# Half of GpSimd's descriptor space given to two more places for expert rows

## The reference, cut to what matters

```python
def peer_ffn(h, wq, sub_keys, u, v):
    def block(t):
        q = (t @ wq).reshape(PEER_BLOCK, PEER_HEADS, 2, PEER_DQ // 2)
        s = jnp.einsum('tpcd,pckd->tpck', q, sub_keys).astype(jnp.float32)
        s1, i1 = lax.top_k(s[:, :, 0], PEER_TOPK)
        s2, i2 = lax.top_k(s[:, :, 1], PEER_TOPK)
        ...
        top, pos = lax.top_k(cand, PEER_TOPK)
        idx = jnp.take_along_axis(cidx, pos, axis=-1)
        g = jax.nn.softmax(top, axis=-1)
        a = jax.nn.gelu(jnp.einsum('tpkd,td->tpk', u[idx], t).astype(jnp.float32), approximate=False)
        return jnp.einsum('tpk,tpkd->td', (g * a).astype(t.dtype), v[idx])
```

## Time and profile before

| | us |
|---|---|
| median of 3 runs | 2861.39 |
| lowest, highest | 2847.32, 2865.62 |
| the profiled execution | 2850.39 |
| its span, first to last instruction | 2848.5 |

### The profile page before, as it was taken

How to read it: one execution, slowest core, us unless ns; L and a number is a source line. 1 busy time by engine, 2 the same in 40 slices (tenths; PEclk the granted TensorE clock), 3 DMA queues, 4 the chain that set the end, 5 groups by cost and what they waited for, 6 DMA issues and landing times.

```text
span 2848.5 us, 43514 instructions
## 1 busy us (share of the span) xinstructions
PE 2307.4 (81%) x16384; PEld 1723.0 (60%) x16384; DVE 1885.7 (66%) x4182; ACT 903.9 (32%) x1615; POOL 1095.7 (38%) x1029
## 2 busy tenths in 40 slices
PE   7999988877455564665757989766999999999998
PEld 5788876445311110113646877523777899997998
DVE  3666885787565666457898877663444587677766
ACT  4556652111100000001023334322423455457544
POOL 0000002544466666667786665676556000000000
PEclk8999999988787776877969999867999999999999
DMA  7432126797799999999999999999999545662554
GB/s 301 151 129 85 38 83 247 279 350 294 289 375 378 365 368 352 358 354 345 409 344 403 401 408 409 408 360 362 363 405 395 208 153 194 190 208 90 186 188 152
DMA packets 225231, 810.32 MB, mean 284 GB/s; under 512 B 24704, under 2 KB 30720, under 8 KB 223232
## 3 DMA queue, kind: packets, MB, share of 16 engines
q0 software_dynamic: 147456, 536.94, 49.3%
q1 hardware_dynamic: 76992, 270.09, 26.5%
q10 hardware_dynamic: 576, 0.52, 0.1%
HBM read 805.35 MB, written 2.10 MB: 283 GB/s over the span
## 4 chain that ended last, share of the span: by engine, by line
PE 39%; DVE 17%; issue 10%; DMA 8%; another core or an unknown queue 6%; POOL 3%; ACT 1%; DVEq 0%; POOLq 0%; SPq 0%; ACTq 0%
PE ps L2005 10%; PE ps L2006 9%; PE ps L2007 9%; DVE pe_ring L2848 6%; PE ps L1940 5%; DMA pe_ring<-in_v,pe_vidx 4%; DMA pe_ring<-in_u,pe_idx 1%; POOL pe_ring L1827 1%; PE ps L1895 1%; DVE pe_itop L2775 1%; POOL pe_ring L1833 1%; DVE la_w_lo L2901 1%; DVE pe_top L2771 1%; DMA la_k<-in_v,pe_vidx 1%
## 5 line engine op out<-in xcount | busy, mean ns | idle before, releaser
L1827 POOL DMA_INDIRECT pe_ring<-in_u,pe_idx x415 | 463.8, 1118 | 293.0 <-issue 113.3
L1940 PE MATMUL ps<-pe_ring,pe_spot 128*32 128x512 f32 x1620 | 386.9, 752 | 199.2 <-DMA pe_ring<-in_v,pe_vidx 140.9
L1833 POOL DMA_INDIRECT pe_ring<-in_v,pe_vidx x405 | 426.5, 1053 | 221.5 <-issue 116.4
L2005 PE MATMUL ps<-la_h_hi,la_w_hi 128*128 128x256 f32 x1696 | 483.4, 285 | 12.1 <-DVE la_w_lo L2901 6.7
L2007 PE MATMUL ps<-la_h_hi,la_w_lo 128*128 128x256 f32 x1696 | 477.8, 282 | 1.7 <-issue 1.7
L2006 PE MATMUL ps<-la_h_lo,la_w_hi 128*128 128x256 f32 x1696 | 477.6, 282 | 1.6 <-issue 1.5
L2901 DVE TENSOR_TENSOR la_w_lo<-la_w_raw,la_w_hi 128x1024 fp32r<-128x1024 f32 (+1 forms) x348 | 415.5, 1195 | 78.0 <-ACT la_w_hi L2470 64.1
L2470 ACT ACTIVATE la_w_hi<-la_w_raw 128x1024 fp32r<-128x1024 f32 (+1 forms) x348 | 359.5, 1033 | 295.4 <-DMA la_w_raw<-in_down 78.7
L2005 PEld LDWEIGHTS ps<-la_h_hi,la_w_hi 128*128 128x128 f32 x1696 | 323.2, 191 | 47.8 <-issue 31.7
L1940 PEld LDWEIGHTS ps<-pe_ring,pe_spot 128*32 128x32 f32 x1620 | 76.9, 125 | 411.9 <-issue 313.1
L2007 PEld LDWEIGHTS ps<-la_h_hi,la_w_lo 128*128 128x128 f32 x1696 | 320.3, 189 | 2.2 <-issue 2.1
(11 more groups left out here) (409 smaller groups left out, 3899.2 us busy)
## 6 DMA issues: line engine op xcount, KB each, us to landing
la_w_raw<-in_gate SPq DMA_DIRECT2D x88, 512.0 KB
la_w_raw<-in_up SPq DMA_DIRECT2D x88, 512.0 KB
la_w_raw<-in_down SPq DMA_DIRECT2D x64, 448.0 KB
la_w_raw<-in_a_in SPq DMA_DIRECT2D x40, 512.0 KB
wring<-in_w_in SPq DMA_DIRECT2D x32, 512.0 KB
la_w_raw<-in_down SPq DMA_DIRECT2D x32, 512.0 KB
wring<-in_wq SPq DMA_DIRECT2D x22, 512.0 KB, 7.5
xT<-in_w_mod_rows SPq DMA_DIRECT2D x8, 1024.0 KB, 4.9
```

The lines of the kernel that those rows point to most:

```text
L1827: pool.indirect_dma_start(row(n), None, io["u"], bass.IndirectOffsetOnAxis(idx[:, t, j:j + 1], 0)).then_inc(land[GATHERS[n][0]], 16)
L1833: pool.indirect_dma_start(row(n), None, io["v"], bass.IndirectOffsetOnAxis(vidx[:, t % 2, at:at + 1], 0)).then_inc(land[GATHERS[n][0]], 16)
L1940: return pe.matmul(ps[PER * grp:PER * grp + PER, half, :], spot[:, j // TOKENS % 2, grp, lo:lo + PER], row(n)[:, half * 512:(half + 1) * 5 ...
L2005: pe.matmul(slot(n), parts_hi[:, n % SPLIT, i, :], hi[:, k, :], start=first, stop=False)
```

## The change

The space for descriptors of GpSimd's dynamic DMAs is 8192 bytes of each partition, and the 8192 bytes that come free hold two further places for gathered rows, `pe_more_rows`, numbers `RING + 10` and `RING + 11`. They are lent from gather 0 to the end and need no wait at their first use (the last test in `slot_free` is cut to the places of `htok`). As each place has a semaphore of its own, three semaphores of the first stage (`x_in`) are now given back at that stage's end and cleared with the others. The diff, whole:

```diff
--- before.py
+++ after.py
@@ -65,6 +65,8 @@
     return [int(np.argmax(bucket >= b)) if (bucket >= b).any() else MAXD for b in range(BUCKETS)] + [MAXD]
 
 
+SCRATCH = 8192
+SPARE = (16384 - SCRATCH) // (4 * D)
 LN_EXP = "natural_log_exp_and_others"
 
 
@@ -244,7 +246,7 @@
                 return (first_ring if m < M_FIRST else later_ring)[m % 4].rearrange("p (k n) -> p k n", n=MODW if m < M_FIRST else D)
 
             c_in, c_ready, mod_dotted = stage_sem("na_c_in"), stage_sem("na_c_ready"), stage_sem("na_mod_dotted")
-            consts_in, x_in, mod_in = sem("consts_in"), [sem(f"x_in{n}") for n in range(3)], [sem(f"mod_in{u}") for u in range(4)]
+            consts_in, x_in, mod_in = sem("consts_in"), [stage_sem(f"x_in{n}") for n in range(3)], [sem(f"mod_in{u}") for u in range(4)]
             padded, silu_ready, x_squared, x_added, x_rooted = [stage_sem(f"na_{x}") for x in ("padded", "silu_ready", "x_squared", "x_added", "x_rooted")]
             mod_used, mod_evac, mod_summed, gained = sem("mod_used"), sem("mod_evac"), sem("mod_summed"), sem("mod_gained")
             x_full, projected_, staged = stage_sem("na_x_full"), stage_sem("na_projected"), stage_sem("na_staged")
@@ -1363,6 +1365,7 @@
     iota16 = sb("pe_iota16", [P, TOPK + 1], on=local)
     HT = T // 2
     work = sb("la_work", [P, 10 * HT], on=local)
+    more_rows = sb("pe_more_rows", [P, SPARE, D], on=local)
     flat = lambda x: x.rearrange("p a n -> p (a n)")
     s_of = [x.rearrange("p (h s n) -> p h s n", h=PE_H, s=2) for x in
             (work[:, 0:2 * D], flat(yT[:, 0:4, :]), flat(yT[:, 4:8, :]), wring[:, 4 * D:6 * D])]
@@ -1502,8 +1505,10 @@
     TOKEN_SLOTS, TOKENS_AT, LENT_AT = [RING + 9, RING + 8, RING + 6, RING + 7], 80, 11
     MORE = [(RING + k, TURN["v", 0, 0], TURN["v", 1, P - 1] + 1) for k in range(4)] + [(RING + 4, 0, KEPT), (RING + 5, 0, KEPT)]
     MORE += [(TOKEN_SLOTS[t], LENT_AT, TOKENS_AT if t else P) for t in reversed(range(TT))] + [(TOKEN_SLOTS[t], TURN["v", t, 16], len(ORDER)) for t in (2, 3)]
+    MORE += [(RING + 10 + k, 0, len(ORDER)) for k in range(SPARE)]
     row_spaces = ([ring[:, k, :] for k in range(RING)] + [within("hT", f"pe_more{k}", k * D, [P, D])[:, :] for k in range(4)]
-                  + [kT[:, :, :].rearrange("p a n -> p (a n)"), v[:, :, :, :].rearrange("p c t n -> p (c t n)"), htok[:, 2, :], htok[:, 3, :], htok[:, 1, :], htok[:, 0, :]])
+                  + [kT[:, :, :].rearrange("p a n -> p (a n)"), v[:, :, :, :].rearrange("p c t n -> p (c t n)"), htok[:, 2, :], htok[:, 3, :], htok[:, 1, :], htok[:, 0, :]]
+                  + [more_rows[:, k, :] for k in range(SPARE)])
     land = [sem(f"pe_land{k}") for k in range(len(row_spaces))]
 
     def slots_of_gathers():
@@ -1814,7 +1819,7 @@
                     pool.wait_ge(first_scored, FIRST)
                 elif FIRST_RING < slot < OUT_RING:
                     pool.wait_ge(first_q, 2 * ((slot - FIRST_RING + 1) // 2))
-                elif n and slot >= RING + 6:
+                elif n and RING + 6 <= slot < RING + 10:
                     pool.wait_ge(dot_done, (slot - RING - 3) * HK)
 
             pool.memset(spot[:, :, :, :], 0.0).then_inc(spot_clear, 1)
@@ -3382,7 +3387,7 @@
     import concourse.bacc as bacc
     from concourse.bass_utils import run_bass_kernel_spmd
 
-    nc = bacc.Bacc("TRN2", target_bir_lowering=False, num_devices=1)
+    nc = bacc.Bacc("TRN2", target_bir_lowering=False, num_devices=1, dynamic_dma_scratch_size=SCRATCH)
     arrays, io = {}, {}
     for name, a in layout(inputs).items():
         arrays[f"in_{name}"] = a
```

## The result

The changed kernel took 2863.5 us (median of 20 runs, 2856.73 to 2875.2), the kernel before 2854.03 on the same chips (20 runs, 2842.29 to 2869.24). The ratio is 1.0033, its 95% interval 1.0019 to 1.0047: 9.5 us slower, where 2.5 us faster was forecast. The time lies inside the range; the sign is wrong. The profiled execution took 2866.3 us.

The account below looks back on a forecast made before the run. Limits differ by stretch: DVE and PE, waits for rows, full DMA engines, GpSimd's pace, then PE. 2850.4 - 12.5 + 10.0 = 2847.9; from the runs' mean, 2856.2 - 2.5 = 2854 us (rounded), range 2824 to 2874.

Parts of the forecast that it names:

- The crawl: Until 745 us, PE, DVE and ACT slow while GpSimd gathers without a break, recovering soon after it stops; cost 10.0 us.
- The cost term: At four stops until 745 us, GpSimd and the other engines' slowdown end 2.5 us later each: 10.0 us.
- The four stops: GpSimd's long stops at 571.8, 627.2, 683.9 and 744.2 us, each expected 2.5 us later.
- the waits at gathers 14 and 28 do not move: Early gathers: borrowed places come at the same gather numbers and keep their waits, so these two waits stay.
- The gains, 12.5 us: From 745 to 1976 us, two more gathers before GpSimd stops for a place save 2.5 + 4.5 + 2.6 + 2.9 us.
- the five priced stops: GpSimd's stops before 772.5, 1019.5, 1139.5, 1423.5 and 1834.7 us, where two more places were to save 12.5 us together.
- The single terms: 2.5 us before 772.5, 4.5 within 783 to 1303, 2.6 at 1400 to 1430, 2.9 at the stop before 1834.7 us.
- The smaller space costs nothing: Descriptor space: 8192 bytes hold an estimated 56 gathers, over twice what the places allow; cost nothing.
- The slower rival: Stops from 783 to 1303 us are the descriptor space being full; half the space adds 66 us, 2920; chance 0.08.
- The faster rival: Stops from 783 to 1303 us are for places; gains 44, net 34 us, time 2822; chance 0.18.
- no gains, full crawl: Whole kernel: upper end of the likeliest case (2844 to 2866, chance 0.70), the added places saving nothing, 2866 us.
- the crawl grows more than the gains: PE needs as long again after a later stop: 2866 and up to 2880 us; chance 0.04.

Follow-up runs that it names:

- e1: Changed kernel without the line lending the two places, descriptor space still 8 KB; ratio to the kernel before 0.9997.
- e3: Changed kernel with the two places lent only for gathers 0 to 127; ratio to the kernel before 1.0017.
- e4: Changed kernel without the lending line; gathers 32 to 127 also wait for the dot of the row 16 before; ratio to the kernel before 0.9952.
- e6: Changed kernel without the lending line; gathers 32 to 127 also wait for the dot of the row 8 before; ratio to the kernel before 0.9937.
- h1: Changed kernel without the lending line; GpSimd clears 480 elements before each of gathers 0 to 147, 120 before 148 to 527; ratio to the kernel before 0.9762.
- e2: Changed kernel with the two places lent only from gather 128 on; ratio to the kernel before 1.0002.
- g1: Changed kernel with the two places lent only for gathers 14 to 127; one run, span 2863.6 us.
- five pairs: Five comparisons of kernels with the two places lent late against kernels lacking them there; mean ratio difference +0.0002.
- g2: e10 with two of the four places in hT not lent (18 rows ahead, not 20, from gather 148 to 527); ratio to the kernel before 0.9895.
- e12: e10 with 120 elements also cleared before each of gathers 148 to 527; ratio to the kernel before 0.9897.
- e8: Changed kernel without the lending line; gathers 32 to 127 bring half rows (2 KB in place of 4); one run, span 2839.7 us.
- e10: e6 with GpSimd clearing 480 elements of a spare tile before each of gathers 112 to 147; ratio to the kernel before 0.9922.

## Why the prediction was wrong

**The crawl, its direction and its size: right.** The cost term was 10.0 us; the first sum is 10.7 us later in the changed kernel, 1.2 in e1. How much of such a delay reaches the end is less sure: e3, which has the early places alone, is 13.1 us late at the first sum and 0.0017, some 5 us, by its ratio. That the crawl grows with the burst and ends behind its end is borne out by e4 to e6, and h1 shows how much of it there is: 66 us at the first sum.

**Its parts: wrong.** The four stops were given 2.5 us each. The last dot of group 0 is 10.3 us late and the first one 4.7, so the three stops between them cost 5.6 us together, and the fourth 0.4 (10.7 less 10.3). (This split is of one trace; e2, which has the fourth alone, is 3.2 us behind e1 at the first sum.) The 4.7 us come from a fifth burst, the first, at 467 to 488 us, of which the prediction says only that "the waits at gathers 14 and 28 do not move". It looked at the long stops and not at the 2.6 us at gather 9, which the two free places removed; g1 shows that the 4.7 hang on it. The waits at gathers 14 and 28 are still there, but end later, at 500.6 and 528.1 us in place of 495.4 and 524.6, and there is one at gather 13 too. That the sum came out near the truth is luck.

**The gains, 12.5 us: the step that failed.** The prediction says "this gains only where GpSimd stops for a place and where its rows are then waited for", and priced such a stop at two gathers. The condition that it left out is that the DMA engines run dry in the stop. These are the five priced stops in the kernel before (columns as in the earlier trace rows):

```profile
744.20:772.40 28.20, 19.92 (x134) 16.32 (x137) 5.67 (x34) 7.19 (x11) 0.01 (x1) 0.75 0.45 165
1016.00:1019.46 3.46, 1.53 (x5) 0.27 (x4) 3.42 (x7) 0.00 (x0) 0.00 (x0) 1.00 1.03 413
1137.20:1139.50 2.30, 2.30 (x16) 0.53 (x12) 1.89 (x13) 0.00 (x0) 0.00 (x1) 0.50 0.93 312
1420.10:1423.50 3.40, 0.00 (x0) 0.00 (x0) 3.37 (x5) 0.00 (x0) 0.00 (x1) 0.50 1.03 413
1828.30:1834.70 6.40, 4.01 (x20) 0.99 (x20) 0.49 (x1) 1.54 (x2) 0.02 (x1) 0.60 1.03 410
```

In three of the five the engines are as full (1.03) as they get and in another nearly so (0.93): a row asked for earlier would have had to wait for the others. Only in the one before the first sum (its term was 2.5 us) are they half idle. The row with 0.96 and 366 GB/s was in hand, read as "all wait for rows"; it also says that the engines had 4% to 7% left (0.96, and 1.03 where they are full), some 20 to 35 us of 520, not the 71 us of GpSimd's stops. The single terms (2.5, 4.5, 2.6 and 2.9 us) are each too small to be measured by themselves; their sum is what the five pairs exclude, with +0.0002 (0.6 us) in place of -0.0035. With the gains at nothing the prediction's own cost term gives +10, and 9.5 was measured.

**The smaller space costs nothing: right** (e1). The slower rival (the space full) falls with it. The faster rival (the stops of 783 to 1303 us are for places) falls with g2 and with e12, which shows them to be for GpSimd's rate. What happened is the upper end of the likeliest case, *no gains, full crawl*: 2866 there, 10 us above its starting point. The rival that was given 0.04, *the crawl grows more than the gains*, wanted the crawl itself to be longer than the sum has it, and it wasn't.

**The Trainium skill** (Runtime: NRT & Kernel Launch, section Instruction fetch mechanics) holds that fetching instructions is hidden, and the prediction drew from it, beside its own sum, one of 2837.9 without the crawl. In the crawl of the kernel before, 556 to 577 us, the DMA queues list no packet of an instruction queue:

```profile
## 3 DMA queue, kind: packets, MB, share of 16 engines
q0 software_dynamic: 2356, 8.60, 102.6%
q1 hardware_dynamic: 2, 0.00, 0.0%
```

TensorE is back at full pace at 577.1 us without one: from 577 to 579.9 us there is none either. And in the crawl of 714 to 745 us there is one of 8 KB, between 717 and 718 us, and the crawl goes on for 27 us behind it:

```profile
q14 instruction: 1, 0.01, 0.1%
```

So no row contradicts the rule on fetching, and the conclusion from it doesn't hold: by h1 the crawl is the gathers' doing. That a fetch delayed in some way that these lists don't show stands behind it was not tested.

**What stays open.** Which resource GpSimd takes from the others at a pitch of 1.24 us and not at 1.62; the runs exclude the DMA engines' bytes (e8) and their fullness (h1), and the queues show no sign of the fetches. Why the transfers behind the first sum stay at 366 GB/s with 0.96 of the engines' time, where other stretches reach 410. And why e10, 43 us ahead at the first sum, is 20 us ahead at the end of its trace and 22 by its ratio, where h1, 66 us ahead at the first sum, is 43 us ahead in its trace and 68 by its ratio: no run took it apart.

## What to carry to other kernels

An engine that runs ahead is not free: before giving a gathering GpSimd more room, look at what the other engines do in its bursts. Single instructions with equal gaps, put down to "issue" on all engines at once, are the sign; slowing GpSimd to a pitch somewhat above that of the transfers (in h1 1.62 us against 1.28 in the early bursts, 1.32 behind) gave 2.4%, more than any number of places that was tried. A stop of the issuing engine is worth only what the DMA engines are idle in it: read their share first, and bound the gain by it.

## What was not expected of the hardware

- GpSimd's gathers at a pitch of 1.24 us (0.94 busy, 0.30 between) slow TensorE to as little as one weight load and matmul every 2.80 us and bring VectorE and ScalarE almost to a stop. It begins some way into a burst: 17 us for VectorE in the one from 539.7 us on, 12 and 15 us for TensorE in those from 661.8 and 698.3 us on. At 1.36 us it is partly so, at 1.62 us not at all in the same stretch, with full DMA engines. TensorE's granted clock from 557 to 575 us is 1.00 in h1, the upper level all through, with the engine busy 18.00 of 18 us; in the earlier trace rows it is 0.78, a mean of both levels, with 10.19 us busy.
- The crawl is the same with 2 KB rows at 211 GB/s as with 4 KB rows at 410.
- A clearing of 480 elements a partition takes GpSimd 0.52 us but moves the next gather by 0.38 only (a pitch of 1.62 in place of 1.24), since the 0.30 us between two gathers shrink to 0.17 behind a clearing.
- A wait added to the engine that feeds all others made the kernel faster (e4: 0.9952).
